# Low parts of ten weight units made by an accumulating DMA instead of VectorE

## The reference

```python
def conv_ffn(h, w_up, conv_w, conv_b, w_down):
    hid = h @ w_up                       # 2048 -> 2 * 5632
    ...                                  # causal convolution of width 3, bias
    gate, up = jnp.split(hid, 2, axis=-1)
    return (jax.nn.gelu(gate, approximate=True) * up) @ w_down   # 5632 -> 2048
```

## Time and profile before

| what | value |
|---|---|
| median of three runs | 2075.25 us (2074.92 to 2076.55) |
| profiled execution, span first to last instruction | 2074.8 us |
| profiled execution beside the fastest run | 2074.8 us of span, 2074.92 us of time |
| TensorE busy | 99% of the span |
| VectorE, ScalarE, GpSimd busy | 70%, 46%, 1% |
| mean granted TensorE clock | 0.999 of full |
| DMA | 393.47 MB, mean 190 GB/s |

### The profile page before, as it was taken

How to read it: one execution, slowest core, us unless ns; L and a number is a source line. 1 busy time by engine, 2 the same in 40 slices (tenths; PEclk the granted TensorE clock), 3 DMA queues, 4 the chain that set the end, 5 groups by cost and what they waited for, 6 DMA issues and landing times.

```text
span 2074.8 us, 26444 instructions
## 1 busy us (share of the span) xinstructions
PE 2063.9 (99%) x10876; PEld 1767.9 (85%) x10876; DVE 1448.6 (70%) x1726; ACT 952.1 (46%) x942; POOL 13.5 (1%) x29
## 2 busy tenths in 40 slices
PE   9999999999999999999999999999999999999999
PEld 7888888878888888878888888888888888888887
DVE  5776786445566767678888645878864778888776
ACT  6544363244534455465554433454443434444642
POOL 0000000000000000000000000000000000000000
PEclk9999999999999999999999999999999999999999
DMA  8756656446566765545655555556565554554463
GB/s 326 223 184 201 175 173 217 159 142 204 161 199 221 253 239 186 180 144 165 209 193 187 199 195 190 181 187 201 181 213 204 160 195 142 176 190 140 143 238 108
DMA packets 304168, 393.47 MB, mean 190 GB/s; under 512 B 16848, under 2 KB 221696, under 8 KB 302896
## 3 DMA queue, kind: packets, MB, share of 16 engines
q1 hardware_dynamic: 300528, 375.02, 55.4%
q0 software_dynamic: 2800, 14.66, 2.0%
q10 hardware_dynamic: 720, 2.11, 0.3%
HBM read 389.66 MB, written 2.10 MB: 189 GB/s over the span
## 4 chain that ended last, share of the span: by engine, by line
PE 95%; DVE 2%; DMA 1%; ACT 1%; issue 1%; SPq 0%; DVEq 0%; ACTq 0%
PE ps L648 91%; PE pm L648 4%; DMA raw<-in_w_in 1%; PE pm L651 1%; DVE wl L1663 1%; ACT wh L1127 0%; DVE cv L1671 0%; ACT xt L1127 0%; DVE xt L1671 0%; DVE up L1820 0%; ACT junk L1147 0%; ACT cv L1127 0%; DVE up L1663 0%; ACT L1127 0%; DVE yM L1663 0%
## 5 line engine op out<-in xcount | busy, mean ns | idle before, releaser
L1663 DVE TENSOR_TENSOR wl<-raw,wh 128x2048 fp32r<-128x2048 f32 (+1 forms) x362 | 803.5, 2227 | 387.6 <-ACT wh L1127 271.9
L1127 ACT ACTIVATE wh<-raw 128x2048 fp32r<-128x2048 f32 (+1 forms) x362 | 669.6, 1859 | 430.5 <-PE ps L648 385.2
L648 PE MATMUL ps<-xt,wh 128*128 128x512 f32 (+1 forms) x2752 | 639.0, 388 | 0.2 <-ACT wh L1127 0.2
L648 PEld LDWEIGHTS ps<-xt,wh 128*128 128x128 f32 (+1 forms) x2752 | 505.9, 188 | 101.5 <-issue 1.3
L648 PE MATMUL ps<-wh,xt 128*128 128x512 f32 x1632 | 397.4, 392 | 2.9 <-ACT wh L1127 1.2
L648 PEld LDWEIGHTS ps<-wh,xt 128*128 128x128 f32 x1632 | 303.9, 188 | 69.3 <-issue 3.6
L648 PEld LDWEIGHTS ps<-xt,wl 128*128 128x128 f32 (+1 forms) x2720 | 338.2, 191 | 7.0
L648 PE MATMUL ps<-xt,wl 128*128 128x256 f32 (+1 forms) x2720 | 340.7, 283 | 0.0
L648 PE MATMUL ps<-wl,xt 128*128 128x512 f32 x816 | 207.4, 390 | 0.6 <-DVE wl L1663 0.6
L648 PEld LDWEIGHTS ps<-wl,xt 128*128 128x128 f32 x816 | 152.8, 188 | 33.8 <-DVE wl L1663 2.1
L1127 ACT ACTIVATE cv<-up,vt 128x256 f32<-128x256 f32 x88 | 52.8, 602 | 234.5 <-DVE up L1663 234.5
(11 more groups left out here) (344 smaller groups left out, 1312.8 us busy)
## 6 DMA issues: line engine op xcount, KB each, us to landing
raw<-in_w_in SPq DMA_DIRECT2D x146, 1024.0 KB, 5.3
raw<-in_ffn_w_up SPq DMA_DIRECT2D x84, 1024.0 KB, 5.1
raw<-in_ffn_w_down SPq DMA_DIRECT2D x40, 1024.0 KB, 5.0
raw<-in_w_out SPq DMA_DIRECT2D x32, 1024.0 KB, 5.4
raw<-in_w_proj_b SPq DMA_DIRECT2D x16, 1024.0 KB, 5.3
raw<-in_w_proj_a SPq DMA_DIRECT2D x8, 1024.0 KB, 5.2
raw<-in_xa_wk SPq DMA_DIRECT2D x4, 1024.0 KB, 5.0
raw<-in_xa_wq SPq DMA_DIRECT2D x4, 1024.0 KB, 4.9
```

Of the source, the lines that this page charges most:

```text
L648: return p.matmul(out, l, r, start=start, stop=stop, skip_group_check=share)
L1127: return a.activation(out, in_, func, bias=bias, scale=scale)
L1663: return v.tensor_tensor(out, a, b, op)
```

## The change

For ten units, the full ones of groups dn01 and dn02, VectorE no longer makes the low part. ScalarE, after it has written the high part, waits for it and for the low slot, and writes the negated high part into `wl`. GpSimd's queue then issues a DMA from `raw` to `wl` that adds the source to what stands in the destination, so that `wl` ends as `raw - wh`. TensorE's low products of such a unit, and the load that reuses its `raw` slot, wait for the DMA's semaphore. The counts of VectorE's semaphore for all later units are lowered by the units left out.

```diff
+ADDED = tuple(("dn0%d" % i, ui) for i in (1, 2) for ui in range(5))
...
+    added = [unit_of[key].n for key in ADDED]
+
+    def low_done(n):
+
+        if n in added:
+            return s_added[n % 3], 16 * sum(m % 3 == n % 3 for m in added if m <= n)
+        return s_lo, hi_count(n) - sum(m < n for m in added)
...
             if begin and u.n > 1:
-                p.wait_ge(s_lo, hi_count(u.n))
+                p.wait_ge(*low_done(u.n))
...
             act(parts(n)[0][:, 0:u.m], raw[s][:, 0:u.m], ACT.Copy).then_inc(s_hi, 1)
+            if n in added:
+                a.wait_ge(s_hi, hi_count(n))
+                a.wait_ge(*low_free(n))
+                act(wl[s][:, 0:u.m], wh[s][:, 0:u.m].bitcast(F), ACT.Copy, scale=-1.0).then_inc(s_neg, 1)
...
         def split_lo(n):
             u, s = units[n], n % 3
+            if n in added:
+                return
...
             if u.n >= 3:
-                e.wait_ge(s_lo, hi_count(u.n - 3))
+                e.wait_ge(*low_done(u.n - 3))
...
         e.wait_ge(*evacuated("wo3"))
         e.dma_start(gb, on_all(I["post_norm_xa"][0])).then_inc(s_gb2, 16)
+
+        for i, n in enumerate(added):
+            e.wait_ge(s_neg, i + 1)
+            e.dma_start(wl[n % 3].bitcast(F), raw[n % 3], accum_op=ALU.add).then_inc(s_added[n % 3], 16)
```

More of the change, by code:

```diff
@@ L462, in build @@
     s_hi, s_lo, s_high, s_used = sem("hi"), sem("lo"), sem("high"), sem("used")
+    s_neg, s_added = sem("neg"), [sem("added%d" % i) for i in range(3)]
     s_acc, s_accfree = sem("acc"), [sem("accfree%d" % i) for i in range(2)]
```

## The result

The changed kernel takes 2100.7 us (median of 4 runs, 2099.94 to 2102.12), the kernel before on the same chip 2075.89. The ratio is 1.0121 with a 95% interval of 1.0109 to 1.0133: 24.8 us slower. The prediction was 2094, with 2087 to 2103 for its forecast. The profiled execution after has a span of 2098.5 us and a time of 2100.32, so about 1.8 us lie around the span. By that offset the span of 2074.8 us of the profile before belongs to the slowest of its runs, 2076.55 us, and not to the fastest. So the profiles are 23.7 us apart and the medians 24.8.

A forecast was written before the change was run, and what follows sets the result against it. TensorE, busy for 99% of the span, was taken as the bound. DMA work of 77.8 us against 61.0 free is 16.8 late, 19 with gaps: 2074.8 + 19 = 2094; forecast range 2087 to 2103, wider range 2075 to 2125.

The forecast's parts named there:

- Nothing to gain on VectorE: In dn01 and dn02, dropping ten subtractions of 2.29 us, 22.9 us on an engine nobody waits for, gains 0 us.
- ScalarE's second copy costs nothing of its own: Ten added copies, 1.92 us each by the nearest row, lie in ScalarE's gaps of 2.16 to 4.38 us: 0 us.
- the ring: Closed turn of a raw slot: load, high copy, negated copy, issue, add; 16.9 us alone against 13.6 to 16.3 us.
- 5.2 us of engine time for an add: Each 1 MiB adding transfer takes 5.2 us of the DMA engines, bounded between 2.6 and 7.8 us.
- Two loads: Basis of the add's price: two reads at a load's pace, the write beside them, 5.2 us; chance 0.42.
- The first adds fit in their time, then each unit waits: In dn01 and dn02: little wait at dn01 0 and 1, then PE idle some 2.4 us for each unit.
- The sum: First issue to last landing: 52.0 us adds, 23.4 loads, 2.4 start and completion, 77.8 against 61.0; 19 with gaps.
- TensorE's clock: Rival: waits of 2.4 us in each changed unit drop TensorE's clock, giving 2105 to 2120; chance 0.06.
- A copy's price and hidden: Rival: an add takes 2.6 us of the engines like a copy and is hidden, 2075 to 2079; chance 0.17.
- a latency-bound ring at a copy's price: Rival: engine time near a copy's but landing after 8.3 us, ring 17.6 us, about +8, 2079 to 2087; chance 0.10.
- The other signs: Trace after: DMA share near 1.0 from 1175 to 1255, loads landing after 7 to 9 us, adds 8 to 13.

The follow-up runs named there:

- no_dma: Changed kernel with the ten transfers deleted and ScalarE's negated copy standing for the low part: 2075.3 us, 0.2 us slower than the kernel before.
- plain_copy: Changed kernel with the ten transfers copying raw to wl instead of adding: 2085.6 us, 10.5 us slower than the kernel before.
- the four units: Changed kernel with adding transfers for only the second and fourth units of dn01 and dn02: 2075.3 us, 0.2 us slower than the kernel before.
- beside_only: Kernel before, plus one copy and ten adding transfers of 1 MiB to an unused tile during dn01 and dn02: 2081.0 us, 5.9 us slower.

## Why the prediction was right, point by point

- **Nothing to gain on VectorE.** Right. no_dma shows it: with VectorE relieved and no transfer the time is that of before.
- **ScalarE's second copy costs nothing of its own.** Right as long as no transfer hangs on it, by the same run. In the ring it is 1.92 us of every turn, as the prediction's 16.9 us have it, and with plain copies leaving it out was worth 9 of 10.5 us.
- **5.2 us of engine time for an add.** Nearly right, 5.5 us, and partly by luck. The sum priced a load at 2.6 us, from its bytes and about 400 GB/s. By the share of the engines' time, the measure by which an add is 5.5 us, a load of 1 MiB took 3.1 us before and 2.9 beside adds; the share of 0.57 in the earlier trace rows says the same. "Two loads" at 2.9 to 3.1 us would have been 5.8 to 6.2 us for an add, and the sum would have come out 28 to 33 us late instead of 19. What an add did cost is two copies: a copy from SBUF to SBUF took 2.6 us in plain_copy. The Trainium skill (Collectives: The Full Stack, section The bandwidth ceiling) gives 1.93 as the ratio of a copy's rate to a reducing transfer's. The trace agrees roughly, with 2.1; the add was somewhat dearer than by that ratio.
- **The first adds fit in their time, then each unit waits.** Right as to the start (dn01 0 and 1 in time). Wrong as to the form: instead of 2.4 us in each unit PE waited in few places, 3.4 to 5.3 us, since the three slots move in step: when one add is late, the load behind it is late, and in SP's queue the two loads behind that. ACT then does three units' copies in a burst (1212.3 to 1223.7).
- **The sum.** The step from the first issue to the last landing was put at 77.8 us of work and 2 to 3 us of gaps, 80.5. The last add landed at 1256.40, where the load that waits for it was issued, so the step took 1256.40 - 1171.80 = 84.6 us. By the shares of that window: ten adds 55 us for 52, loads 24 for 23.4, 2.4 us of start and end, and 3 us of gaps for 2.7. The loads come out right by two errors that cancel: 2.9 us each and not 2.6, but 8.4 of them and not 9. The add's price is the most of the difference. Against the 61.0 us that were free the step is 23.6 us late, for the 19 of the prediction.
- **TensorE's clock.** The prediction gave its fall 0.06 and named it as a sign of being wrong in kind. It fell three times, each time behind a wait (the earlier trace rows show the one of before), so in this the prediction was wrong, though the time that it gave didn't hang on it. The argument against it, 70% busy throughout, failed because the waits come in lumps: from 1190 to 1195 us PE was busy for 2.02 of 5 us. But the price was small. The matmuls of the stretch took 9.3 us more, and most of that lies in time in which the next low part wasn't there yet: the chain above holds no piece of PE from the first add up to 1250.05. What can be counted as the clock's own is the end: the last low products started 1258.22 - 1256.40 = 1.8 us behind the last add. The Trainium skill (TensorE: Matmul & The Clock Gate, section HAM oscillation) says that waits for data between bursts of matmuls put the array back at half rate again and again. The trace agrees: three of PE's five waits for the adds, those of 3.36, 5.25 and 5.26 us, were followed by matmuls at half clock.
- **The rivals.** "A copy's price and hidden" was wrong twice: an add isn't a copy, and even copies are not hidden (2085.6). The rival of a latency-bound ring at a copy's price, forecast at about +8, is what plain_copy then showed (+10.5, and +1.6 once a turn is 1.95 us shorter). It was the wrong limit for adds and the right one for copies, though with a copy's landing at 7.4 us (median) and not 8.3.
- **The other signs.** PE's waits released by the DMA, the idle time of ACT ahead of the high copies and the 352 low parts of VectorE came as said, and behind the stretch the span is the same 812.8 us in both profiles. The engines' share was 0.98 to 0.99 up to 1236 us and then 0.88, not near 1.0 up to 1255. Loads landed after 4.5 to 15.4 us (said: 7 to 9), adds after 7.0 to 14.2 (said: 8 to 13).
- **The total.** The 425 matmuls from 1166.0 us on took 96.0 us before; after they run from 1164.2 to 1285.7, 121.5 us. That is 25.5 us more: 16.2 us of idle time of PE (15.7 for adds, 0.5 for a high part) and 9.3 us of slower matmuls (8.3 over the whole span, as PE was busy for 1.0 us less ahead of the stretch). It is also the 23.6 us of the step and the 1.8 us behind it. The span grew by 23.7 only, since the profile after reached the stretch 1.8 us earlier than the one before, which has nothing to do with the change.

## What to carry to other kernels

A DMA that computes isn't free of charge because the engines are half idle: price it in their time (here an add of 1 MiB took 5.5 us, a copy 2.6, a load 2.9 to 3.1), add it to the loads of the same stretch, and compare with the time TensorE takes for a unit; above that the loss grows with every unit; below it, it can be free, as the four units were. Then count the turn of a buffer: a transfer that must end before the buffer can be loaded again is part of a ring, and a ring can stall engines that are at 0.83. And look at what stands in a queue ahead of such a transfer; one load that waited for another engine cost 8 us.

## What the runs showed of the hardware that was not expected

- An adding transfer of 1 MiB from SBUF to SBUF held its engines for 5.5 us and landed 7.0 us after its issue when alone, 8.9 as the median of the ten; a copy 2.6, 4.4 (the shortest) and 7.4 us. GpSimd's issue took 0.85 us for an add and 0.53 for a copy.
- Splitting it into pieces of 2 KB instead of 8 KB raised the engines' time of an add from 5.5 to 6.4 us; the time of the kernel didn't change beyond the intervals.
- Behind PE's waits of 3.36, 5.25 and 5.26 us the next eight matmuls ran at 1.2 GHz; behind those of 0.55 and 1.29 us in the same stretch they didn't (2.11 us for eight). The length of the wait alone doesn't decide it: before, the clock fell behind one of 2.10 us, and in plain_copy it stayed up behind one of 2.8.
- A DMA share of 0.99 with loads landing after 8.4 instead of 5.0 us cost PE nothing in beside_only, where the low parts and the raw slots didn't wait for the adds.
